# Mixture of experts: a ring of seven rooms in the first quad, the residual added in the fourth quad, the loop turned by one expert

## What is computed

```python
def hier_moe(x, w_group, b_group, w_expert, b_expert, w_gate_up, w_down):
    ...   # each token picks 1 of 4 groups and 2 of its 8 experts: 32 experts, 512 assignments
    def expert_block(args):
        xb, e = args
        gate, up = jnp.split(xb @ w_gate_up[e], 2, axis=-1)     # 1024 x 1024
        return (jax.nn.silu(gate) * up) @ w_down[e]             # 512 x 1024
    ...
ffn = hier_moe(x, ...)
x = layer_norm(DN_ALPHA * x + ffn, ln2_g[l], ln2_b[l])          # the residual
```

## Time and profile before

| | us |
|---|---|
| median of 3 runs (lowest, highest) | 1828.28 (1826.84, 1829.95) |
| the profiled execution's own time | 1824.51 |
| its span | 1822.7 |
| granted TensorE clock over the span, share of full speed | 0.987 |
| TensorE busy | 1760.8 (97%) |
| VectorE busy | 1079.8 (59%) |
| ScalarE busy | 709.8 (39%) |

### The profile page before, as it was taken

How to read it: one execution, slowest core, us unless ns; L and a number is a source line. 1 busy time by engine, 2 the same in 40 slices (tenths; PEclk the granted TensorE clock), 3 DMA queues, 4 the chain that set the end, 5 groups by cost and what they waited for, 6 DMA issues and landing times.

```text
span 1822.7 us, 32010 instructions
## 1 busy us (share of the span) xinstructions
PE 1760.8 (97%) x12588; PEld 1427.8 (78%) x12588; DVE 1079.8 (59%) x1923; ACT 709.8 (39%) x1127; POOL 21.2 (1%) x26
## 2 busy tenths in 40 slices
PE   9999999999999999998999999997999999999996
PEld 8999989889999999997899999996953333333332
DVE  6775566687755877668787657867762222222223
ACT  5444453454344544455644446854321101110111
POOL 0000000000000000000000001000020000000000
PEclk9999999999999999999999999998999999999999
DMA  5545333345453355541255545442859999999995
GB/s 232 184 166 207 112 139 139 38 160 177 168 212 135 139 184 193 194 145 47 93 184 184 200 172 184 155 149 89 347 215 415 419 427 429 427 428 428 427 428 215
DMA packets 42337, 409.67 MB, mean 225 GB/s; under 512 B 5304, under 2 KB 5304, under 8 KB 7056
## 3 DMA queue, kind: packets, MB, share of 16 engines
q1 hardware_dynamic: 40032, 402.21, 56.9%
q0 software_dynamic: 1936, 5.79, 1.5%
q10 hardware_dynamic: 288, 0.52, 0.1%
HBM read 405.87 MB, written 2.63 MB: 224 GB/s over the span
## 4 chain that ended last, share of the span: by engine, by line
PE 81%; DVE 10%; DMA 6%; ACT 1%; issue 1%; DVEq 0%; SPq 0%; ACTq 0%
PE ps L596 79%; DMA late<-w_gate_up 6%; PE ps L600 2%; DVE w_lo L1611 1%; DVE h L1717 1%; DVE x_lo L1673 1%; DVE h L1721 1%; DVE rs L1653 1%; DMA raw<-w_units 1%; DVE arena L1975 1%; DVE arena L1895 0%; DVE small L1981 0%; DVE arena L2003 0%; DVE arena L2123 0%; ACT w_hi L1227 0%
## 5 line engine op out<-in xcount | busy, mean ns | idle before, releaser
L596 PE MATMUL ps<-x_hi,w_hi 128*128 128x256 f32 (+1 forms) x2144 | 619.7, 289 | 12.7 <-DVE x_lo L1671 4.5
L596 PE MATMUL ps<-x_lo,w_hi 128*128 128x256 f32 (+1 forms) x2144 | 613.5, 286 | 0.0
L596 PE MATMUL ps<-x_hi,w_lo 128*128 128x256 f32 (+1 forms) x2144 | 611.9, 285 | 0.0
L1611 DVE TENSOR_TENSOR w_lo<-raw,w_hi 128x1024 fp32r<-128x1024 f32 (+1 forms) x352 | 441.2, 1292 | 76.9 <-ACT w_hi L1227 76.6
L596 PEld LDWEIGHTS ps<-x_hi,w_hi 128*128 128x128 f32 x2144 | 407.1, 190 | 23.5 <-issue 9.5
L1227 ACT ACTIVATE w_hi<-raw 128x1024 fp32r<-128x1024 f32 (+1 forms) x352 | 379.5, 1111 | 111.0 <-PE ps L596 86.0
L596 PEld LDWEIGHTS ps<-x_hi,w_lo 128*128 128x128 f32 x2144 | 408.8, 191 | 0.0
L596 PEld LDWEIGHTS ps<-x_lo,w_hi 128*128 128x128 f32 x2144 | 408.0, 190 | 0.2
L596 PE MATMUL ps<-hid_hi,w_hi 128*128 128x272 f32 (+1 forms) x720 | 206.0, 286 | 0.7 <-DVE hid_lo L1673 0.3
L596 PE MATMUL ps<-hid_hi,w_lo 128*128 128x272 f32 (+1 forms) x720 | 204.6, 284 | 0.0
L596 PE MATMUL ps<-hid_lo,w_hi 128*128 128x272 f32 (+1 forms) x720 | 204.0, 283 | 0.0
(11 more groups left out here) (328 smaller groups left out, 1990.4 us busy)
## 6 DMA issues: line engine op xcount, KB each, us to landing
raw<-w_units SPq DMA_DIRECT2D x144, 1024.0 KB, 4.8
soon<-w_gate_up SPq DMA_DIRECT2D x33, 2048.0 KB, 20.0
late<-w_gate_up SPq DMA_DIRECT2D x31, 2048.0 KB, 18.3
raw<-w_out_units SPq DMA_DIRECT2D x32, 1408.0 KB, 6.0
soon<-w_down SPq DMA_DIRECT2D x16, 2048.0 KB, 20.4
late<-w_down SPq DMA_DIRECT2D x16, 2048.0 KB, 19.7
bias_rows<-kT POOLq DMA_DIRECT2D x1, 1536.0 KB, 33.4
cst<-table SPq DMA_DIRECT2D x1, 1448.0 KB, 11.9
```

What stands on the lines that cost most here:

```text
L596: return nc.tensor.matmul(out_ap, lhsT, rhs, start=start, stop=stop, skip_group_check=True)
L1611: v.tensor_tensor(part(w_lo, c, 0, n), raw_slot(u, j * n, n), part(w_hi, c, 0, n).bitcast(F32), ALU.subtract).then_inc(lo_made, 1)
```

## The change

1. The seven rooms are a ring for the pieces of the first four experts: piece k goes to room k mod 7, where piece k-7 was, and SP waits for one begun piece fewer. This holds for pieces 7 to 13. From piece 14 on six of the rooms are in use and the waits are as before (`loop_rooms`). `PIECE_PARTS` = 1 means that a piece is still one DMA, with the same rows of 16 KB.
2. SP has six experts written out instead of four; its loop starts at the fourth pair.
3. TensorE's and ScalarE's loops are turned by one expert: three blocks of quad 0 are written out, the loop's body is the fourth block of one quad and three blocks of the next, and the last block stands behind the loop, without gathers. ScalarE leaves the copies of that gather (`gathered`) out as well.
4. The residual leaves quad 0. TensorE's loop is split in two at quad 4 (`NE // 8`), and the four products of the residual stand between them, behind the third block of quad 3.
5. The last `combine` adds the high part as soon as it is there (`yhi_made`), and the low part behind the wait for `evac[7]`.

```diff
-        piece_ahead = soon[:, 0:PIECE]
-        pieces = {at: (late if early is None else soon)[:, n * PIECE:(n + 1) * PIECE]
-                  for at, early, n in (((0, 1), True, 1), ((0, 2), True, 2), ((1, 0), True, 3),
-                                       ((1, 1), None, 0), ((1, 2), None, 1), ((0, 0), None, 2))}
+        piece_rooms = [soon[:, n * PIECE:(n + 1) * PIECE] for n in range(4)] + [late[:, n * PIECE:(n + 1) * PIECE] for n in range(3)]
+        N_ROOMS = len(piece_rooms)
+        loop_rooms = [(4 * EXP_UNITS + n) % N_ROOMS if n < 2 else n - 1 for n in range(2 * EXP_UNITS)]
...
-            load_expert(2, 0, 0, of=(1, 2))
-            load_expert(3, 1, EXP_UNITS)
+            for piece in range(7, 6 * EXP_UNITS):
+                e, i = divmod(piece, EXP_UNITS)
+                if e < 4:
+                    load_piece(e, i, piece % N_ROOMS, PIECE_PARTS * (piece - 7) + 2)
+                else:
+                    n = piece % (2 * EXP_UNITS)
+                    load_piece(e, i, loop_rooms[n], PIECE_PARTS * (piece - (7 if e == 4 and n < 2 else 6)) + 2)
...
-                if s == 3:
+                if s == 3 and gathers:
...
-            for s in range(4):
+            def quads(first, end):
+
+                with pe.Fori(first, end) as quad:
+                    expert(quad - 1, 3)
+                    for s in range(3):
+                        expert(quad, s)
+
+            for s in range(3):
                 expert(0, s)
-                if s >= 2:
-                    p = s - 2
-                    pe.wait_ge(x2_ready, p + 1)
-                    for n in range(2):
-                        mm(ps[2 * p + n][:, :], m_alpha, m_o[:, p * D + n * 512:p * D + (n + 1) * 512], False, False)
             pe.wait_ge(count_ready, 1)
             n_quads = pe.value_load(meta_i[0:1, MAXB:MAXB + 1], min_val=NE // 4, max_val=MAXB // 4)
-            with pe.Fori(1, n_quads) as quad:
-                for s in range(4):
-                    expert(quad, s)
+            quads(1, NE // 8)
+            for p in range(2):
+                pe.wait_ge(x2_ready, p + 1)
+                for n in range(2):
+                    mm(ps[2 * p + n][:, :], m_alpha, m_o[:, p * D + n * 512:p * D + (n + 1) * 512], False, False)
+            quads(NE // 8, n_quads)
+            expert(n_quads - 1, 3, False)
+            pe.wait_ge(yhi_made, 4 * n_quads)
+            for p in range(2):
+                combine(3, (p,), m_y[0:1])
             pe.wait_ge(evac[7], E_BASE[7] + 4 * n_quads)
             for p in range(2):
-                combine(3, (p,)).then_inc(y_done, 1)
+                combine(3, (p,), m_y[1:2]).then_inc(y_done, 1)
```

More of the change, by code:

```diff
@@ L499, in _, with load_piece @@
                 last_row = row + n
-            def load_piece(e, i, dst, done):
+            def load_piece(e, i, room, begun=None):
                 src = w_gate_up[bass.ds(e, 1), 4 * P * i:4 * P * (i + 1), :] if i < 2 else w_down[bass.ds(e, 1), :, :]
-                sp.dma_start(dst, src.rearrange("a (p k) n -> p (a k n)", k=4)).then_inc(done, 16)
-            def load_expert(e, slot, begun=None, of=range(EXP_UNITS)):
-                for i in of:
+                src = src.rearrange("a (p k) n -> p a k n", k=4)
+                n = 4 // PIECE_PARTS
+                for g in range(PIECE_PARTS):
@@ L509, in load_expert @@
                     if begun is not None:
-                        sp.wait_ge(exp_begun, begun + i + 2)
-                    load_piece(e, i, pieces[slot, i], e_landed[slot * EXP_UNITS + i])
-            def first_loads(j):
+                        sp.wait_ge(exp_begun, begun + g)
+                    sp.dma_start(piece_rooms[room][:, g * n * D:(g + 1) * n * D].rearrange("p (a k n) -> p a k n", a=1, k=n),
+                                 src[:, :, g * n:(g + 1) * n, :]).then_inc(e_landed[room][g], 16)
@@ L515, in first_loads, with load_ahead @@
+            def load_ahead(piece):
+                load_piece(piece // EXP_UNITS, piece % EXP_UNITS, piece % N_ROOMS)
+            for j in range(N_UNITS - last_units):
+                load(0, last_row + j, last_units + j)
                 if j == 0:
                     sp.wait_ge(x_ready, 11 * KT)
[L517 to L521, removed]
@@ L538, in _ @@
                 for j in range(2):
                     e = sp.value_load(meta_i[0:1, bass.ds(2 * pair + j, 1)], min_val=0, max_val=NE - 1)
-                    load_expert(e, j, 2 * EXP_UNITS * pair + EXP_UNITS * (j - 2))
+                    for i in range(EXP_UNITS):
+                        n = j * EXP_UNITS + i
+                        load_piece(e, i, loop_rooms[n], PIECE_PARTS * 2 * EXP_UNITS * pair + PIECE_PARTS * (n - 6) + 2)
             for p in range(2):
@@ L1110, in gather, with combine @@
                 m.then_inc(g_full, 1)
-            def combine(s, ps_of=(0, 1)):
+            def combine(s, ps_of=(0, 1), ys=m_y):
                 for p in ps_of:
@@ L1116, in combine, with expert, arrived @@
                         hs = slice(64 * n, 64 * n + 64)
-                        for y in m_y:
+                        for y in ys:
                             m = mm(ps[2 * p + n][:, :], m_pT[s % 2][hs, p * P:(p + 1) * P], y[hs, :], False, False)
                 return m
-            def expert(quad, s):
-                b, r = 4 * quad + s, s % 2
-                use = 32 * quad + 16 * (s // 2) + 16
+            def expert(quad, s, gathers=True):
+                b = 4 * quad + s
+                def arrived(i, g):
+                    piece = EXP_UNITS * s + i
+                    if isinstance(quad, int):
+                        room, use = piece % N_ROOMS, 16 * (piece // N_ROOMS + 1)
+                    else:
+                        room = loop_rooms[piece % (2 * EXP_UNITS)]
+                        use = 32 * quad + 16 * (piece // (2 * EXP_UNITS)) + (16 if 4 * EXP_UNITS - N_ROOMS > room else 0)
+                    pe.wait_ge(e_landed[room][g], use)
+                    return piece_rooms[room]
                 pe.wait_ge(evac[5], E_BASE[5] + b)
                 for i in range(2):
[L1127 to L1132, removed]
                     for kk in range(4):
+                        if kk % (4 // PIECE_PARTS) == 0:
+                            weights = arrived(i, kk * PIECE_PARTS // 4)
                         k = 4 * i + kk
@@ L1174, in expert @@
                             m = mm(ps[7][64 * n:64 * n + 64, :], m_hT[:, kk * P + 64 * i:kk * P + 64 * i + 64],
-                                   pieces[r, 2][:, a:a + 512], k == 0, k == 3)
-                            if k == 0 and n == 0:
+                                   weights[:, a:a + 512], k == 0, k == 3)
+                            if k % (4 // PIECE_PARTS) == 0 and n == 0:
                                 m.then_inc(exp_begun, 1)
```

51 lines of the change are left out of this document (28 added, 23 removed).

## The result

| | before | after |
|---|---|---|
| median (lowest, highest), us | 1827.56 (1825.09, 1829.95) | 1815.24 (1812.95, 1816.36) |
| runs | 4 | 4 |
| the profiled execution's own time, us | 1824.51 | 1812.95 |
| its span, us | 1822.7 | 1811.1 |

The ratio of after to before is 0.9944, with a 95% interval of 0.9927 to 0.9961: 7 to 13 us faster. The forecast was 1821.5 us, 6.8 us faster, within 1818.0 to 1825.3.

A forecast was written before the change was run, and what follows sets the result against it. Weight loads bound the kernel by 2.3 us a quad, followed by a tail. Stream 2.8, code -0.3, last block 4.0 and combine 0.3 sum to 6.8 us: 1828.3 - 6.8 = 1821.5 us, range 1818.0 to 1825.3.

The forecast's parts named there:

- The seven rooms alone: Early weight stream: piece 7 issued 5.8 us earlier, lead gone by piece 16, so nothing gained at the stream's end.
- Those are the times of now: Pieces 14 and 16, seven rooms alone: their waits are the old ones, so landings not before 1396.2 and 1410.0 us.
- The residual out of quad 0: TensorE starts quad 1 3.8 us earlier, later issues follow, and the stream comes 2.8 us earlier, with or without the rooms.
- the sum: Pieces 14 to 19: each lands at the later of stream and issue; piece 19 at 1423.6 instead of 1426.4 us.
- The rooms then only cover what else delays the stream: Before piece 16: beside the residual's gain, the rooms only absorb other delays such as a code block, up to 1.4 us.
- The residual in quad 3: Its 3.8 us of TensorE return where TensorE waits for loads anyway; 8.8 us of cover, so cost nothing.
- More code: Full stream: some 2.5 more 16 KB code blocks share the DMA engines; cost 0.3 us, bounds 0 and 2.8.
- the first rival: Stream gains nothing, through code blocks or another empty queue; only the tail's 4.3 us remain, 1824.0 us; chance 0.18.
- the last (code that queues behind the weights): Seam behind quad 3 and last block: two code fetches each 21.9 us late, 32 us slower, 1860; chance 0.03.
- The last block: Program's end: without the gathers the last product with down starts at about 1801.4 instead of 1805.37, 4.0 us earlier.
- the combine in two: VectorE at the end: high products done beforehand, two left ahead of the statistics; 0.3 us gained, bounds 0 and 0.5.
- The base: Starting time for the subtraction: 1828.3 us, median of runs shown, 3.8 us above the profiled execution's 1824.5.

The follow-up runs named there:

- before_again: The kernel before, unchanged, measured and profiled a second time; ratio 1.0007 to before, 476.3 us from the mark (start of piece 0's first product) to the end.
- before_third: The kernel before, unchanged, a third profile; ratio 0.9995 to before, 476.1 us from the start of piece 0's first product to the end.
- without_rooms: The changed kernel with the six rooms and waits of before, keeping its loops, residual and tail; ratio 0.9954 to before, 469.5 us from mark to end.
- after_again: The changed kernel, unchanged, measured and profiled a second time; ratio 0.9942 to before, 467.8 us from mark to end.
- after_third: The changed kernel, unchanged, a third profile; ratio 0.9962 to before, 467.8 us from mark to end.
- without_tail: The changed kernel with the last block's gathers and the one combine of before, keeping rooms and residual; ratio 0.9976 to before, 472.1 us from mark to end.
- rooms_only: The kernel before with only the ring of seven rooms and its waits; ratio 1.0006 to before, 476.3 us from mark to end.

## Why the prediction was off

**What bounds the kernel: right.** A full stream at 427 to 428 GB/s, whose phase (by how much all its later landings are shifted) is set early, and a tail. Only the place at which the phase is set was taken too early, see below.

**The seven rooms alone: right.** Forecast nothing, measured 1.0006 and 476.3 us. "Those are the times of now" holds for the issues alone: piece 14 landed at 1399.9 before, brought by the stream, not at 1396.2.

**The residual out of quad 0: right in kind, too small together with the rooms.** Forecast 2.8 us for both and 2.8 for the residual alone; measured 4.2 for both and 2.7 alone. The failed step is "16 at 1400.1 + 8.8 (the median of the earlier trace rows) = 1408.9, issue", carried to the end of the stream one for one, since "the stream's phase is thus fixed at pieces 16 to 19". Counted from the mark, these are the landings of four pieces:

| kernel | 16 issued | 16 landed | 19 landed | 21 landed | last landed |
|---|---|---|---|---|---|
| before | 55.4 | 63.8 | 79.9 | 91.0 | 453.8 |
| before_again | 55.4 | 63.8 | 79.8 | 91.2 | 454.0 |
| before_third | 55.4 | 64.5 | 80.3 | 91.1 | 453.9 |
| without_rooms | 53.3 | 63.5 | 78.2 | 88.5 | 451.3 |
| the sum, with rooms | 53.5 | 62.3 | 77.0 | | 451.3 |
| after | 53.1 | 60.8 | 75.5 | 86.8 | 449.6 |
| after_again | 53.2 | 61.2 | 75.9 | 86.8 | 449.7 |
| after_third | 53.2 | 62.1 | 76.8 | 86.8 | 449.6 |
| without_tail | 53.2 | 62.4 | 77.1 | 86.9 | 449.7 |

In the first profile of the change piece 16 took 7.7 us in place of 8.8, which seems to be the whole error. It is not, and that it fits is luck: in after_third the piece took 8.9 us and in without_tail 9.2, piece 19 landed where the sum had it, and the stream ended 4.1 to 4.2 us earlier all the same. Pieces 16 and 21 of after_third:

```profile
L509 SPq DMA_DIRECT2D soon<-w_gate_up x1: 328/328/328, 1397.6 to 1397.6; - x1
...
DMA to landing us min/median/max: 8.9/8.9/8.9
...
L509 SPq DMA_DIRECT2D soon<-w_gate_up x1: 338/338/338, 1417.7 to 1417.7; - x1
...
DMA to landing us min/median/max: 13.5/13.5/13.5
```

Between executions of one kernel the landing of piece 19 differs by up to 1.3 us, that of piece 21 by 0.1; and from piece 21 to the last it is 362.8 us in before and after alike. So in these kernels the phase is fixed at piece 21, not at 16 to 19, and there the change is worth 4.2 to 4.3 us.

The trace shows how. A load reports its landing in sixteen parts, and the piece has landed with the last. Of piece 16 fifteen parts are there 7.5 to 7.7 us after the issue in all four profiles with rooms and without the residual in quad 0. Only the sixteenth is late, by 0.2 to 1.5 us. One block of code begins to load at 53.3 to 53.8 us, and another at 81.8 to 82.5. Behind the second, most parts of piece 21 land by 85.1 to 85.4 us and the last at 86.8 or 86.9. A part that had been late since piece 16 is no later than that, so two delays on different parts do not add. Before, most parts of piece 21 land by 89.4 to 89.7 and the last 1.4 to 1.6 us behind them. The sum took the landing of a last part for the pace of the whole queue. Two of the four landings of the earlier trace rows, pieces 18 and 19 (9.3 and 9.5), stood in line besides. With 7.6 us for piece 16 and its issue 0.4 us earlier than forecast, the sum gives 2.8 + 1.2 + 0.4 = 4.4 us; measured 4.2. That the late parts are those that shared an engine with code is argued: the trace shows the blocks and the late parts, not the engine of either.

"The rooms then only cover what else delays the stream" fell short with it: with six rooms it is the stream, not the issue, that sets when piece 16 lands. In without_rooms it was issued at 1399.73, also 53.3 us after the mark, and landed 10.2 us later, at 63.5:

```profile
L504 SPq DMA_DIRECT2D late<-w_gate_up x1: 333/333/333, 1399.7 to 1399.7; - x1
...
DMA to landing us min/median/max: 10.2/10.2/10.2
```

At piece 21 it is 88.5 against 86.8 with seven rooms, and those 1.7 us are left at the end of the stream: the seventh room's worth, where the prediction had 0 and up to 1.4 for a block of code.

**The residual in quad 3: right.** Forecast no cost with 5 us of cover left: the shortest time from issue to landing in the full stream is 15.2 us after, where 18.3 - 3.8 = 14.5 was the forecast, and a piece needs no more than 9.5. The residual stood at 1548.6, 205.3 us from the mark, and not near 1560.

**More code: size wrong by 0.3.** The DMA queues of the changed kernel in 1345:1462, and from there to 1788:

```profile
q8 instruction: 4, 0.07, 0.2%
...
q8 instruction: 2, 0.03, 0.0%
```

Two code blocks came in the full stream, about as forecast, and a third at 1790.5, while the last piece loads. They cost nothing: from piece 21 to the last it is 362.8 us in before, where one block came (at 114 us), and 362.8 in each profile of after. In the profile of after they delayed parts that were 1.7 us ahead of the last one. In rooms_only a block at 113.8 us makes piece 26 land 6.6 us behind piece 25 instead of 4.9, and takes back the 1.3 us that this kernel was ahead at piece 21. So the price taken for a block (1.4 us if it falls on the last part) was near the right size, and that none fell there is luck. TensorE has no gap at the seam (the residual at 1548.62 follows the product before it at once, whose row ends at 1548.68). So neither the first rival (no gain in the stream) nor the last (code that queues behind the weights) came about. The Trainium skill (Runtime: NRT & Kernel Launch, section Instruction fetch mechanics) says that a taken branch to code outside the window held on chip stalls the engine until that code is fetched. At the new branch into the second loop the trace shows no stall: the residual's eight records end at 1552.32 and the next product starts at 1552.25. Whether that code was on chip already it does not show; the two blocks were loaded 17 and 46 us after the start of the residual.

**The last block: right** (4.0 forecast, 3.9 measured), **the combine in two: right** (0.3, measured 0.24).

**The base: the second failed step.** It is "the median of the runs shown is 3.8 us higher, so I forecast 1828.3 - 6.8". The time missed the forecast by 6.3 us, and only 1.5 of it is the gain (8.3 where the sum had 6.8). The rest is the base. Five later medians of before are 1823.6 to 1825.4 us, about the 1824.5 of the profiled execution, and 1824.5 - 8.3 = 1816.2 would have been within 1 us of the measured 1815.24. With the gain put right, the forecast from 1828.3 would have been 1820.0, still 4.8 us too high. Times like 1828 are those of executions of before at a clock of 0.981 to 0.983; the four first executions of after all had 0.986 to 0.988. The clock of the four of before beside them is not on record, so that they were such executions is likely, not shown.

## What to carry to other kernels

Where a stream of loads ends a program, look for the last place at which its queue runs empty: only what moves that place moves the end. Check in a second profile from which load on the landings repeat; here it was piece 21, five pieces behind the one that the sum was built on. A landing is that of the last of many parts, so one of them does not give the pace of the queue. An edit that gains nothing alone (one more buffer) can be worth something once another has moved the bound that hid it, so try them together and undo each. And before a few microseconds are believed, measure the same stretch, mark to mark, in two profiles of one program, and compare whole times at the same granted clock.

## What the runs showed of the hardware

- A stretch of this program repeats to 0.2 us in three executions (476.1 to 476.3, and 467.8 three times), while the 1340 us ahead of it vary by 2.2 us in three executions of before.
- Loads of 1 MB in rows of 8 KB moved 420 GB/s in a queue that was always full, loads of 2 MB in rows of 16 KB 427 to 428 GB/s, both with the engines' busy share at 1.01. Rows and number of DMAs changed together.
- The time of a whole execution goes with its granted TensorE clock: 1828.2 us (median of 22) at 0.981 to 0.983, 1823.8 us (median of 58) at 0.986 to 0.988, the same program.
- A load of 2 MB issued when the queue was empty (piece 7) landed 7.5 to 7.8 us later in eleven of the twelve profiles with whole pieces there, 8.4 us in the other.
- A load reports its landing in sixteen parts, and in a full stream a late part stays late: in after the last part stands 1.7 us behind the others from piece 21 to piece 30.
